# Expert weights in 8 KB pieces, slots released in pairs, and the gather at the beginning of its gang

## The reference

```python
combine = one_hot(group)[:, :, None] * e_w[:, None, :]      # top-1 of 4 groups, top-2 of its 8 experts
for gi in range(N_GROUPS):                                  # 4 x 8 = 32 experts
    hid = silu(einsum('nd,edf->nef', xt, w_gate[gi])) * einsum('nd,edf->nef', xt, w_up[gi])
    out = out + einsum('nef,efd->nd', hid * combine[:, gi, :, None], w_down[gi])
```

## Time and profile before

| | us |
|---|---|
| median of 3 runs (1819.49 to 1824.91) | 1823.59 |
| the profiled execution | 1827.08 |
| its span, first to last instruction | 1825.4 |
| PE busy (share of the span) | 1458.4 (80%) |
| DVE busy | 413.3 (23%) |
| ACT busy | 259.1 (14%) |

### The profile page before, as it was taken

One profiled execution on the slowest core, in us unless ns is written; L12 is line 12 of the kernel. 1 busy time (PEld: TensorE's weight loads), 2 busy tenths in 40 slices (PEclk: granted clock), 3 DMA queues, 4 the chain that ended last, 5 costly groups with the idle time before them and its releaser, 6 DMA issues.

```text
span 1825.4 us, 21730 instructions
## 1 busy us (share of the span) xinstructions
PE 1458.4 (80%) x9078; PEld 755.6 (41%) x9078; DVE 413.3 (23%) x954; ACT 259.1 (14%) x502; POOL 116.0 (6%) x266
## 2 busy tenths in 40 slices
PE   8999999899776677667699898998997657665763
PEld 6675457453222122212375555475543212221220
DVE  1134332251100110011411343313421011101104
ACT  2222112210000000000121311122000000000000
POOL 5222200000000000000020110100000000000000
PEclk9999999999888898889799887999999989989997
DMA  8434745859999999999633434367869999999993
GB/s 294 139 117 135 203 172 180 344 209 369 409 410 410 409 409 410 410 410 409 222 102 129 141 100 164 106 238 286 318 253 409 409 410 410 410 409 410 410 410 134
DMA packets 167249, 535.17 MB, mean 293 GB/s; under 512 B 5582, under 2 KB 23054, under 8 KB 167184
## 3 DMA queue, kind: packets, MB, share of 16 engines
q1 hardware_dynamic: 163296, 522.08, 74.2%
q0 software_dynamic: 2160, 5.89, 1.1%
q10 hardware_dynamic: 1728, 6.29, 1.0%
HBM read 521.75 MB, written 12.49 MB: 293 GB/s over the span
## 4 chain that ended last, share of the span: by engine, by line
PE 52%; DMA 32%; SPq 9%; DVE 3%; ACT 2%; issue 1%; ACTq 0%; DVEq 0%; POOL 0%
PE ps L648 12%; SPq L444 9%; DMA scr<-in_w_gate 8%; PE ps L703 7%; PE ps L682 6%; DMA W<-in_w_gate 6%; PE ps L976 6%; DMA scr<-in_w_up 5%; PE ps L956 4%; DMA W<-in_w_up 4%; DMA MEMB<-in_w_gate 4%; DMA W<-in_w_down 3%; PE ps L663 2%; PE ps L796 2%; PE ps L815 1%
## 5 line engine op out<-in xcount | busy, mean ns | idle before, releaser
L976 PE MATMUL ps<-W,scr 128*32 128x512 f32 x1536 | 213.7, 692 | 126.0 <-DMA W<-in_w_gate 68.3
L648 PE MATMUL ps<-XT,W 128*128 128x288 f32 x896 | 229.1, 419 | 3.5 <-ACT XT L1066 2.2
L648 PEld LDWEIGHTS ps<-XT,W 128*128 128x128 f32 x896 | 174.7, 196 | 54.6 <-ACT XT L1066 3.0
L1594 DVE TENSOR_TENSOR scr<-scr,ps 128x512 f32<-128x512 f32 x16 | 11.0, 688 | 750.0 <-PE ps L976 750.0
L976 PE MATMUL ps<-scr 128*32 128x512 f32 x768 | 109.2, 698 | 85.1 <-DMA scr<-in_w_up 30.2
L976 PEld LDWEIGHTS ps<-W,scr 128*32 128x32 f32 x1536 | 46.9, 121 | 273.8 <-DMA W<-in_w_gate 101.3
L956 PE MATMUL ps<-scr,X 128*128 128x128 f32 (+1 forms) x864 | 158.7, 314 | 0.0
L956 PEld LDWEIGHTS ps<-scr,X 128*128 128x128 f32 (+1 forms) x864 | 122.7, 194 | 50.7 <-issue 16.5
L976 PE MATMUL ps<-MEMB,scr 128*32 128x512 f32 x768 | 102.5, 675 | 29.6 <-DMA MEMB<-in_w_gate 29.6
L682 PE MATMUL ps<-W,MEMB 128*128 128x512 f32 x256 | 116.5, 609 | 0.8 <-ACT MEMB L1093 0.8
L976 PEld LDWEIGHTS ps<-scr 128*32 128x32 f32 x768 | 23.2, 121 | 166.4 <-DMA scr<-in_w_gate 44.6
(11 more groups left out here) (288 smaller groups left out, 1343.0 us busy)
## 6 DMA issues: line engine op xcount, KB each, us to landing
W<-in_w_gate SPq DMA_DIRECT2D x32, 2048.0 KB, 23.8
W<-in_w_up SPq DMA_DIRECT2D x32, 2048.0 KB, 23.7
W<-in_w_down SPq DMA_DIRECT2D x32, 2048.0 KB, 23.9
scr<-in_w_gate SPq DMA_DIRECT2D x16, 2048.0 KB, 23.8
MEMB<-in_w_up SPq DMA_DIRECT2D x16, 2048.0 KB, 23.6
scr<-in_w_down SPq DMA_DIRECT2D x16, 2048.0 KB, 23.8
MEMB<-in_w_gate SPq DMA_DIRECT2D x16, 2048.0 KB, 23.6
scr<-in_w_up SPq DMA_DIRECT2D x16, 2048.0 KB, 24.1
```

What stands on the lines that cost most here:

```text
L648: last = mm(bank[:, 0:NT], w[:, k, c * P:(c + 1) * P], XT[:, k, :], start=(k == 0), stop=(k == KC - 1))
L976: last = mm(ps[j * CAP:(j + 1) * CAP, bank, :], x[:, k, j * CAP:(j + 1) * CAP], w[:, j, i, c * HALF:(c + 1) * HALF], start=(part % 4 == 0 ...
```

## The change

A unit now holds two experts instead of four, with half of the contraction instead of a quarter, so that each expert's part in a partition is 8 KB, contiguous in HBM. Two units (the two halves of the gang) form a pair; PE waits for both, works through both and counts `unit_done` once for the pair. SP waits for pairs accordingly. The order in which contraction rows lie in partitions changes with it: the gather reads X with a step of 4 words instead of 2, and the transposes of HS read with a step of 2. Gather stands at the beginning of its own gang, also for the first, behind the wait for the number of rounds; DVE therefore makes that number straight after the first one-hots. All of scatter stands between gate and up pairs, and DVE adds its parts ahead of the product. `keep_warm` gets a bank and is called behind the gather (1), behind each up pair (2) and ahead of each down pair (2).

```diff
+    PAIRS = UNITS // 2
 ...
-        gate_rows = I["w_gate"].rearrange("l g e (u p k) f -> u p (l g e) (k f)", u=4, p=P)
-        down_rows = I["w_down"].rearrange("l g e (u p) d -> u p (l g e) d", p=P)
+        gate_rows = I["w_gate"].rearrange("l g e (u p k) f -> u p (l g e) (k f)", u=2, p=P)
+        down_rows = I["w_down"].rearrange("l g e (u p k) d -> u p (l g e) (k d)", u=2, p=P)
 ...
-                    sp.wait_ge(S(f"unit_done{l - 1}"), rm1 * (GANGS * UNITS) + (GANGS * UNITS - RING + r + 1))
+                    sp.wait_ge(S(f"unit_done{l - 1}"), rm1 * (GANGS * PAIRS) + (GANGS * PAIRS - RING // 2 + r // 2 + 1))
 ...
-                    part, e = n % UNITS, bass.ds(gang * GANG + l * NE, GANG)
-                    rows = (gate_rows, up_rows, down_rows)[part // 4][part % 4]
-                    sp.dma_start(ring_slot(l, n % RING).rearrange("p (j n) -> p j n", j=GANG), rows[:, e, :]).then_inc(S(f"ring{n % RING}_in{l}"), 16)
+                    part = n % UNITS
+                    e = bass.ds(gang * GANG + l * NE + part % 2 * (GANG // 2), GANG // 2)
+                    rows = (gate_rows, up_rows, down_rows)[part // 4][part % 4 // 2]
+                    sp.dma_start(ring_slot(l, n % RING).rearrange("p (j n) -> p j n", j=GANG // 2), rows[:, e, :]).then_inc(S(f"ring{n % RING}_in{l}"), 16)
 ...
-                        sp.wait_ge(S(f"unit_done{l}"), ii * (2 * UNITS) + (n + 1))
+                        sp.wait_ge(S(f"unit_done{l}"), ii * (2 * PAIRS) + (n // 2 + 1))
 ...
-                    return X[0:ROWS[t], t, :].rearrange("t (u p k) -> t u p k", u=KC // 2, k=2)
+                    return X[0:ROWS[t], t, :].rearrange("t (u p k) -> t u p k", u=2, k=KC // 2)
 ...
-                gather(0)
                 pe.wait_ge(S("rounds_known"), count_at("rounds_known", l, 1))
 ...
+                def pair(n, turn, x, banks):
+                    part, r = n % UNITS, n % RING
+                    per = KC // 2 if part < 8 else 2
+                    w = [ring_weights(l, n + half, per) for half in range(2)]
+                    u = part % 4 // 2
+                    for half in range(2):
+                        pe.wait_ge(S(f"ring{r + half}_in{l}"), turn * (16 * 2 * UNITS // RING) + 16 * (n // RING + 1))
+                    for k in range(per):
+                        for c, bank in enumerate(banks):
+                            for j in range(GANG):
+                                last = mm(ps[j * CAP:(j + 1) * CAP, bank, :], x[:, u * per + k, j * CAP:(j + 1) * CAP],
+                                          w[j // 2][:, j % 2, k, c * HALF:(c + 1) * HALF], start=(u == 0 and k == 0),
+                                          stop=(u == 1 and k == per - 1))
                     last.then_inc(S(f"unit_done{l}"), 1)
 ...
+                            gather(it)
+                            pe.wait_ge(S(f"ht{l}"), it + 1)
+                            keep_warm(1, 2)
                             pe.wait_ge(S(f"xg_a{l}"), it + 1)
                             pe.wait_ge(S(f"xg_d{l}"), it + 1)
-                            pe.wait_ge(S(f"ht{l}"), it + 1)
-                            for u in range(4):
-                                unit(odd * UNITS + u, turn, XG, [2])
-                            gather(it + 1)
-                            pe.wait_ge(S(f"h_ready{l}"), it + 1)
-                            for u in range(4):
-                                unit(odd * UNITS + 4 + u, turn, XG, [3])
+                            for u in (0, 2):
+                                pair(odd * UNITS + u, turn, XG, [2])
                             pe.wait_ge(S(f"y_sb{l}"), it + 1)
                             pe.wait_ge(S(f"pwt_sb{l}"), it + 1)
-                            scatter(it, range(0, 3))
+                            scatter(it, range(SCATTERS))
+                            pe.wait_ge(S(f"h_ready{l}"), it + 1)
+                            for u in (0, 2):
+                                pair(odd * UNITS + 4 + u, turn, XG, [3])
+                                keep_warm(2, 1)
 ...
-                            scatter(it, range(3, SCATTERS))
 ...
-                            for u in range(4):
-                                unit(odd * UNITS + 8 + u, turn, HT, [4, 5])
+                            for u in (0, 2):
+                                keep_warm(2, 1)
+                                pair(odd * UNITS + 8 + u, turn, HT, [4, 5])
 ...
                 one_hots(slice(0, GANG))
+                dve.wait_ge(S("counts"), count_at("counts", l, 1))
+                step(red(small[:, 11, 0:1], ps[:, 5, TT * NE:(TT + 1) * NE], AX.X, ALU.max))
+                step(ts(THR, iota[:, 1:1 + (NT - 1) // CAP], float(CAP), small[:, 11, 0:1], ALU.mult, ALU.is_lt))
+                step(red(small[:, 12, 0:1], THR, AX.X, ALU.add))
+                tell(cp(rounds[:], small[0:1, 12, 0:1]), S("rounds_known"))
 ...
-                        tt(HS, SG, ps[:, 3, :], ALU.mult).then_inc(S(f"h_ready{l}"), 1)
-                        move_gathered(it + 1)
                         for n in range(SCATTERS):
                             dve.wait_ge(S(f"scat{l}"), it * SCATTERS + (n + 1))
                             add_scattered(n)
+                        dve.wait_ge(S(f"sg{l}"), it + 1)
+                        dve.wait_ge(S(f"unit_done{l}"), it * PAIRS + 4)
+                        tt(HS, SG, ps[:, 3, :], ALU.mult).then_inc(S(f"h_ready{l}"), 1)
```

More of the change, by code:

```diff
@@ L260, in ring_weights @@
         def ring_weights(l, n, per):
-            return ring_slot(l, n % RING).rearrange("p (j k n) -> p j k n", j=GANG, k=per)
+            return ring_slot(l, n % RING).rearrange("p (j k n) -> p j k n", j=GANG // 2, k=per)
         def wslot(l, name):
@@ L485, in _ @@
                     for n in range(2 * UNITS):
-                        sp.wait_ge(S(f"unit_done{l}"), ii * (2 * UNITS) + (n + 1))
+                        sp.wait_ge(S(f"unit_done{l}"), ii * (2 * PAIRS) + (n // 2 + 1))
                         load_unit(n + RING, (ii * 2 + (n + RING) // UNITS) % GANGS)
                 for n in range(2 * UNITS - RING):
-                    sp.wait_ge(S(f"unit_done{l}"), rm1 * (GANGS * UNITS) + ((GANGS - 2) * UNITS + n + 1))
+                    sp.wait_ge(S(f"unit_done{l}"), rm1 * (GANGS * PAIRS) + ((GANGS - 2) * PAIRS + n // 2 + 1))
                     load_unit(n + RING, GANGS - 2 + (n + RING) // UNITS)
@@ L897, in attention, with keep_warm @@
                 pe.wait_ge(S("oa_ready"), count_at("oa_ready", l, 3))
-            def keep_warm(n):
+            def keep_warm(n, bank=0):
                 for _ in range(n):
-                    mm(ps[:, 0, :], ones[:], X[:, 0, 0:HALF], start=True, stop=True)
+                    mm(ps[:, bank, :], ones[:], X[:, 0, 0:HALF], start=True, stop=True)
             def logits(l, t):
@@ L945, in scatter, with rows_of_x @@
                         last.then_inc(S(f"scat{l}"), 1)
-                def pairs_of_x(t):
-                    return X[0:ROWS[t], t, :].rearrange("t (u p k) -> t u p k", u=KC // 2, k=2)
+                def rows_of_x(t):
+                    return X[0:ROWS[t], t, :].rearrange("t (u p k) -> t u p k", u=2, k=KC // 2)
                 def gather(it):
@@ L955, in gather @@
                         for t in range(TT):
-                            last = mm(ps[:, k // 4, (k % 4) * P:(k % 4 + 1) * P], pairs_of_x(t)[:, k // 2, :, k % 2],
+                            last = mm(ps[:, k // 4, (k % 4) * P:(k % 4 + 1) * P], rows_of_x(t)[:, k // 4, :, k % 4],
                                       PG[0:ROWS[t], t, :, :].rearrange("p j c -> p (j c)"), start=(t == 0), stop=(t == TT - 1))
@@ L960, in gather @@
                     last.then_inc(S(f"xg_ps1{l}"), 1)
-                gather(0)
                 pe.wait_ge(S("rounds_known"), count_at("rounds_known", l, 1))
                 rm1 = pe.value_load(rounds[0:1, 0:1], min_val=0, max_val=ROUNDS - 1)
-                def unit(n, turn, x, banks):
+                def pair(n, turn, x, banks):
                     part, r = n % UNITS, n % RING
[L970 to L973, removed]
+                    per = KC // 2 if part < 8 else 2
[4 more added lines that the diff above has]
+                    for k in range(per):
                         for c, bank in enumerate(banks):
                             for j in range(GANG):
-                                last = mm(ps[j * CAP:(j + 1) * CAP, bank, :], x[:, k, j * CAP:(j + 1) * CAP],
-                                          w[:, j, i, c * HALF:(c + 1) * HALF], start=(part % 4 == 0 and i == 0),
-                                          stop=(part % 4 == 3 and i == len(ks) - 1))
+                                last = mm(ps[j * CAP:(j + 1) * CAP, bank, :], x[:, u * per + k, j * CAP:(j + 1) * CAP],
+                                          w[j // 2][:, j % 2, k, c * HALF:(c + 1) * HALF], start=(u == 0 and k == 0),
+                                          stop=(u == 1 and k == per - 1))
```

(8 more changed lines are left out.)

9 lines of the change are left out of this document (2 added, 7 removed).

## The result

The changed kernel takes 1831.3 us (median; 1829.45 to 1834.26), the kernel before 1823.59 beside it: a ratio of 1.0043 [1.0023, 1.0063] (the brackets hold a 95% interval, here and below). It is slower by 0.4%, where 1805 was forecast in a range from 1797 to 1823. The profiled execution took 1832.01 us, with a span of 1830.2, 4.8 more than before.

The account below looks back on a forecast made before the run. The prediction took DMA of expert weights to bound the kernel's two expert stages. Pieces -28.2, stage starts +7.2 and ends +2.1 made -18.9 us on 1823.6, so 1805 us, range 1797 to 1823.

Parts of the forecast that it names:

- The 8 KB pieces: Expert weight loads: a piece takes 310 ns, a unit 4.96 us instead of 5.12; 28.2 us gained over both layers.
- The first rival: Weight loads: pieces are cut to 4 KB or cost two of them, pairs' edges remain; 1833 us, slower; 13%.
- The strided reads: Gather's stationary operand, step 4 instead of 2: cost taken as 0, bound +17.6 us in all.
- the second rival: Gather: the step of 4 slows the stationary load, +8.8 us on each layer's first gather; 1822 us, no change; 8%.
- Pairs at the start: Start of each layer's expert stage: later gather, constant matmul and later first release cost +3.6 us a layer, +7.2 for both.
- The prediction's own sign of being wrong: Among the stated signs of error: a gather on PE takes more than 9 us, where 8.8 was forecast.
- Pairs at the end: After each stage's last landing: 32 records in 3.6 us instead of one unit; together +2.1 us, up to +5.5.
- The steady stage: Mid-stage gangs: PE's chain of 47 to 49 us stays below DMA's 59.5, so added work is hidden.
- the third rival: Steady gangs: PE becomes the bound with the array below full clock, 64.1 us a gang; 1879 us, slower; 4%.
- slack that I had counted: Steady gangs: room between PE's chain of 47 to 49 us and DMA's 59.5 us.
- The next layer's loads: Dense loads and memory rows leaving after the last pair: 13.4 us and a transfer's latency, hidden with some 10 us to spare.
- The sum: Whole kernel: -28.2 + 7.2 + 2.1 = -18.9 us, giving 1805 us.

Follow-up runs that it names:

- the third experiment: The changed kernel with units of four experts x 4 KB again, so a step of 2 in X, pairs and constant matmuls kept: 1846.23 us.
- the eighth experiment: The changed kernel, step of 4 kept, with four constant matmuls instead of one ahead of the wait for the number of rounds: 1830.8 us.
- the first experiment: The changed kernel with X copied once a layer by ACT into an order in which gather reads contiguously: 1825.02 us.
- the seventh experiment: The changed kernel with X copied into contiguous order and four constant matmuls instead of one ahead of the wait for the rounds: 1810.81 us.
- the sixth: The changed kernel with gather one gang ahead, the first ahead of the wait for the rounds, step of 4 kept: 1846.91 us.
- the kernel with all three edits: The changed kernel with X contiguous, four constant matmuls at the wait for the rounds, six ahead of the last down pair: 1808.3 us.

## Why the prediction was wrong, by its own steps

**The 8 KB pieces: right.** 310 ns were forecast, 311 measured, and the third experiment, with pieces of 4 KB, loses the gain again (12.1 us a stage); 5.12 - 119.42 / 24 = 0.144 us a unit, times 176, is 25.4 of the 28.2. The remaining 1.4 us to the measured 24.0 lie at the edges of the stages and were not followed. The single instruction fetch of the earlier trace rows was a good stand-in. The first rival, pieces cut to 4 KB, is out, and with it the sum that followed from reading the Trainium skill's packet size (DMA: Bandwidth & Descriptors, SWDGE vs HWDGE vs iDMA) as a cut.

**The strided reads: the step that failed, with its rival at 8%.** I took 0 "by the nearest row", a step of 2, and kept +17.6 as the bound. The load went from 196 to 327 ns at full clock, and gather is paced by it: 48 x 327 ns are 15.7 us, and it took 15.2 to 15.9. That is +7 us on each first gather, near the second rival's +8.8, and the eighth experiment shows that the step alone is enough for it. The rival's time, 1822, still falls short: the last pairs cost 5.4 us more than it has, and the pieces gave 4.2 less. The Trainium skill (SBUF — State Buffer, Door 1: The DMA port swizzle) wants two hits in each line of 16 bytes. By that rule step 1 and 2 run at full speed and step 4 does not; the trace agrees: 186 to 192, 187 to 197 and 303 to 332 ns at full clock. The same section of the Trainium skill also calls a stride of up to 4 fp32 free; with a step of 4 the trace does not agree, and the measurement decides.

**Pairs at the start: the times of its waits were right, what they do to the clock was missing.** Gather was forecast to start at 401.5 and started at 401.57; the register load behind the number of rounds (made at 400.18) is in that time. That the two agree so closely is part luck: from the router's last constant matmul it is 2.8 us forecast and 3.15 measured. But I priced the idle time ahead of gather as 1.7 us and left "gather itself 8.8 us as before". Behind those 2 us the clock fell to 0.50 and stayed there through the gather, and at 0.50 even a contiguous load takes 333 ns. The constant matmul and a part of the first pair then ran at the low clock too: 2.08 us where 1.10 stood, and 4.31 and 5.47 where I had 3.6 for the warm array. The kernel before had no idle time there, and its clock stayed at 1.00 for the whole gather. That the idle time makes the clock fall is shown where X is contiguous (the first against the seventh experiment); with the step of 4 it falls either way. In the kernels that keep the array warm and read X contiguously the start is 17.0 us in both layers, 2.3 and 3.9 more than before: 6.2, where 7.2 was forecast.

The two causes hide each other. A strided load takes the same time at both clocks, and a contiguous one at half clock takes as long as a strided one; whoever removes one of them finds the other at nearly the same price. The strided stream also brings the clock down by itself (the sixth and eighth experiments). Why it does was not tested. The prediction's own sign of being wrong, a gather above 9 us, came true.

**Pairs at the end: mis-sized.** I summed PE's work behind the last up landing to 17 of 20 us, called the last idle "short" and took 3.6 us a pair. The idle was 4.4 to 4.5, the clock fell (0.56 in the window from 866 on), and the pairs took 6.1 and 6.6: +7.5 in place of +2.1. The bound of +5.5, from 5.3 us a pair, was below that. With the idle filled the pairs are 3.64, the forecast size.

**The steady stage: right, with little left.** The period is DMA's, and PE still waits for landings (3.21 us ahead of the pair at 507.73, 1.43 and 1.29 ahead of two in the next gang), so the third rival is out. But the chain of waits now gives PE 70% and DMA 23%: gathers of 15.4 us take 6.6 of the 10.5 to 12.5 us of slack that I had counted.

**The next layer's loads: hidden, as forecast.** PE's first matmul on them stands 26.5 us behind the last pair's end (872.39 to 898.86), as before, and waits for ACT. My sum of 13.4 us for them is 14.9 with its 1.5 us of latency, which changes nothing.

**The sum.** With step and clock mended the account of the prediction holds: -24.0 + 6.2 + 2.1 = -15.7, and the kernel with all three edits measures 1808.3 - 1823.4 = -15.1 us. That is inside the predicted range; the kernel that was asked about is not.

## What to carry to other kernels

A new access step on the stationary operand of a matmul stream whose loads set its pace needs a price of its own, and where no row has one, the upper bound should weigh in the forecast and not only in the range. Where a change puts a wait ahead of PE work on the path that sets the end, ask what the idle time does to the clock of the work behind it, not only how long it is. When one repair shows little, try it together with the other suspect before you dismiss either.

## What the hardware showed that I had not expected

- Load of a stationary operand of 128 columns in float32: step 1, 190 ns at full clock and 333 at half (the first experiment); step 2, 196 (the kernel before) and 331 (the third); step 4, 327 and 325 (the eighth). Of these three only step 4 does not depend on the clock.
- Behind 2.15 us without work a contiguous gather fell to 0.50 and was still there at its end, 11 us on, though PE was busy throughout (the first experiment); with that time filled the same instructions kept 1.00 (the seventh).
- An unbroken gather at step 4 fell from 1.00 to 0.50 on its way with no idle time in it (the eighth experiment: 1.00 at its start at 402.40, 0.50 from 408 on; the sixth likewise).
